# The projection slab of the decay rates two places earlier, its tables beside the last gate slabs, and the first convolution tap on ScalarE

## What is computed

```
hin  = x * (1 + scale) + shift                      # adaLN
proj = hin @ w_in                                   # 1024 -> 3072 (q,k,v) + 1024 (gate z) + 8 (b) + 8 (a)
qkv, hist = causal_dwconv(proj[:3072], conv_hist, conv_w)     # 4 taps per channel, over time
q, k, v = split(silu(qkv));  q, k = l2_normalize(q)/sqrt(128), l2_normalize(k)
beta = sigmoid(b);  g = -exp(a_log) * softplus(a + dt_bias)   # the rates, per token and head
G = cumsum(g) in each chunk                                   # decays: exp(G), exp(G_last - G), exp(G_i - G_j)
per chunk: solve (I + A) u = ..., with A from beta, k k^T and the decays; update the state S; o = ...
o = rms_norm(o) * silu(z);  out = o @ w_out
```

## Time and profile before

| | us |
|---|---|
| median of the runs | 3310.03 |
| the profiled execution's own time | 3313.34 |
| its span | 3311.8 |
| PE busy in it | 3096.9 (94%) |
| DVE busy | 1899.9 (57%) |
| ACT busy | 1074.6 (32%) |
| POOL busy | 925.7 (28%) |

### The profile page before, as it was taken

How to read it: one execution, slowest core, us unless ns; L and a number is a source line. 1 busy time by engine, 2 the same in 40 slices (tenths; PEclk the granted TensorE clock), 3 DMA queues, 4 the chain that set the end, 5 groups by cost and what they waited for, 6 DMA issues and landing times. The chain is left out here.

```text
span 3311.8 us, 51171 instructions
## 1 busy us (share of the span) xinstructions
PE 3096.9 (94%) x18908; PEld 2889.9 (87%) x18908; DVE 1899.9 (57%) x2897; ACT 1074.6 (32%) x2084; POOL 925.7 (28%) x648
## 2 busy tenths in 40 slices
PE   6999987999999999999998979989799999999995
PEld 2999985999988999999997867767789999999994
DVE  3899974777636545555547654434255555454555
ACT  1222223555426222222223634333144222222224
POOL 0322224566323322222222121010214222222222
PEclk8999997999999999999999989999899999999998
DMA  4444562221111111111110110000201111111111
GB/s 203 167 166 165 195 239 98 62 57 38 39 37 34 46 50 44 44 44 44 44 44 28 53 46 26 27 33 20 92 26 45 45 44 44 44 44 44 44 38 54
DMA packets 85016, 220.28 MB, mean 67 GB/s; under 512 B 9244, under 2 KB 40804, under 8 KB 83748
## 3 DMA queue, kind: packets, MB, share of 16 engines
q1 hardware_dynamic: 40692, 137.05, 12.3%
q10 hardware_dynamic: 44208, 81.66, 7.5%
HBM read 189.94 MB, written 28.75 MB: 66 GB/s over the span
## 5 line engine op out<-in xcount | busy, mean ns | idle before, releaser
L334 PE MATMUL PS<-HH,WH 128*128 128x354 f32 (+1 forms) x3336 | 1098.9, 329 | 78.7 <-issue 21.4
L338 PE MATMUL PS<-HH,WL 128*128 128x354 f32 (+1 forms) x3336 | 1091.1, 327 | 0.0
L337 PE MATMUL PS<-HL,WH 128*128 128x354 f32 (+1 forms) x3336 | 1090.4, 327 | 0.0
L330 POOL TENSOR_TENSOR WL<-RAW,WH 128x1024 fp32r<-128x1024 f32 x193 | 508.8, 2636 | 1054.5 <-ACT WH L325 1054.5
L334 PEld LDWEIGHTS PS<-HH,WH 128*128 128x128 f32 x3336 | 636.4, 191 | 94.4 <-issue 79.3
L337 PEld LDWEIGHTS PS<-HL,WH 128*128 128x128 f32 x3336 | 636.6, 191 | 1.8
L338 PEld LDWEIGHTS PS<-HH,WL 128*128 128x128 f32 x3336 | 635.0, 190 | 0.0
L1790 DVE SCALAR_TENSOR_TENSOR X<-PS,ADA,X 128x354 f32<-128x354 f32 (+1 forms) x704 | 329.8, 491 | 438.0 <-PE PS L338 437.5
L325 ACT ACTIVATE WH<-RAW 128x1024 fp32r<-128x1024 f32 x199 | 211.0, 1060 | 544.0 <-PE PS L334 543.7
L334 PE MATMUL PS<-FH,WH 128*128 128x354 f32 (+1 forms) x960 | 326.5, 340 | 9.9 <-DVE X L1790 9.8
L1765 DVE SCALAR_TENSOR_TENSOR CF<-UF,PSF,CF 128x1060 f32<-128x1060 f32 x176 | 331.6, 1939 | 0.0
(11 more groups left out here) (298 smaller groups left out, 4206.3 us busy)
## 6 DMA issues: line engine op xcount, KB each, us to landing
RAW<-ws SPq DMA_DIRECT2D x199, 512.0 KB, 3.6
ADR<-wada ACTq DMA_DIRECT2D x72, 512.0 KB, 4.9
scr<-V ACTq DMA_DIRECT2D x32, 530.0 KB, 3.6
AD<-wada SPq DMA_DIRECT2D x4, 2048.0 KB, 23.8
X<-xT SPq DMA_DIRECT2D x1, 4240.0 KB, 17.2
OUTT<-scr SPq DMA_DIRECT2D x1, 4240.0 KB, 14.6
scr<-OH ACTq DMA_DIRECT2D x8, 530.0 KB, 2.7
ADG<-wada SPq DMA_DIRECT2D x2, 2048.0 KB, 11.5
```

Of the source, the lines that this page charges most:

```text
L330: e.tensor_tensor(WL[u][:, :], RAW[:, u, :], WH[u][:, :].bitcast(fp32), ALU.subtract).then_inc(lo_done, 1)
L334: mm = e.matmul(out, WH[w][:, c:c + 128], mh, start=first, stop=False)
L337: e.matmul(out, WH[w][:, c:c + 128], ml, start=False, stop=False)
L338: return e.matmul(out, WL[w][:, c:c + 128], mh, start=False, stop=last)
```

## The change

Four things, all in the first 600 us.

1. **The first tap.** ACT computes CV = U·w0 (an activation Copy with the tap as scale) right after it has copied U and before it splits WH. DVE keeps the other three taps.
2. **The order of slabs.** The b and a slab is put at place 30; the last two gate slabs are 31 and 32. The tables are made under slabs 31 and 32: PE's transposes stand between the first and second chunk of slab 31, its sums between the same chunks of slab 32, the GCN transpose ahead of the last chunk of slab 32. The banks of the tables change (5, 6, 7 and 3). The order of ACT, DVE and POOL follows.
3. **Loads.** SP also issues KF and QE of chunk 2, ahead of gsc and ADG; ACT no longer does at chunk 0. The gsc store stands ahead of ADG. The load of S0 by ACT is put after the GAM activations of chunk 0, and both it and `vec_init(0)` wait for the stores of the last gate slabs.
4. **Places in SBUF**: AB over U, GTR a tile of its own.

```diff
+S_AB = QKVB + ZB - 2
...
             load_kq(sp, 1)
+            load_kq(sp, 2)
+            sp.wait_ge(gx, 9)
+            sp.dma_start(gsc, GTR[0:8 * (GT + 1), :]).then_inc(gt_st, 16)
             need(sp, up_done, 3 * (QKVB + ZB) + 3)
...
-                        if i + 2 <= LAST:
+                        if 1 <= i <= LAST - 2:
                             load_kq(a, i + 2)
...
+                    if not z:
+                        need(act, pst_rdy, n + 1)
+                        need(act, up_ev, 3 * n + 3)
+                        act.activation(CV[u][:, :], UB[u][:, GAP - (GC - 1):GAP - (GC - 1) + T], ACT.Copy, scale=PST[:, u, 0:1]).then_inc(tap_rdy, 1)
...
+            load_ada(act, S_AB, 0, True)
             for ch, (c0, cw) in enumerate(CHS):
-                need(act, up_done, 3 * n + ch + 1)
+                need(act, up_done, 3 * S_AB + ch + 1)
                 act.activation(AB[:, c0:c0 + cw], PS[:, ch, 0:cw], ACT.Copy).then_inc(up_ev, 1)
+                if ch == 0:
+                    load_ada(act, S_AB + 1, 1, True, 3)
+            split_hi(act, S_AB + 2, 0)
...
-                    v.tensor_scalar(CV[u][:, :], src(0), PST[:, u, 0:1], None, ALU.mult).then_inc(vec_ch, 1)
...
+            vec_ada_sums(v, S_AB, 0, S_AB // 2, True)
...
             v.tensor_tensor(GX[:, 1], GX[:, 1], GX[:, 3], ALU.subtract).then_inc(bg_rdy, 1)
+            vec_ada_sums(v, S_AB + 1, 1, S_AB // 2, True)
             need(v, gx, 4)
...
+            def to_tokens(ch):
+                if ch == 1:
+                    need(pe, up_ev, 3 * (S_AB + 1))
...
+                if ch == 2:
+                    need(pe, gx, 1)
+            dense(pe, S_AB + 1, 1, S_AB + 1, 1, to_tokens)
+
+            def decays(ch):
+                if ch == 1:
+                    need(pe, bg_rdy, 6)
...
+                if ch == 2:
+                    pe.wait_ge(bg_rdy, 9)
...
+                    pe_gt(pe)
+            dense(pe, S_AB + 2, 0, S_AB + 2, 0, decays)
```

More of the change, by code:

```diff
@@ L1199, in act_gdn @@
             act_gam(a, 0, 1)
+            for u in range(2):
+                need(a, v_st[u], 16 * (QKVB + ZB) // 2)
+            a.dma_start(SS0[:, :, :], s0).then_inc(s0_ld, 16)
             act_vb(a, 0)
@@ L1376, in vec_gdn @@
             vec_aq(v, 0)
+            for u in range(2):
+                need(v, v_st[u], 16 * (QKVB + ZB) // 2)
             vec_init(v, 0)
@@ L2565, in _, with gate @@
                 body(i, False)
-            with act.Fori(QKVB // 2, (QKVB + ZB) // 2 - 1) as i:
+            need(act, tail_rdy, QKVB)
+            act.dma_start(o_gcv, TAIL[:, :, :, :]).then_inc(out_done, 16)
+            with act.Fori(QKVB // 2, S_AB // 2) as i:
                 body(i, True)
-            body((QKVB + ZB) // 2 - 1, True, True)
-            n = QKVB + ZB
+            def gate(n, u, b):
+                need(act, v_st[u], 16 * (b // 2))
+                for ch, (c0, cw) in enumerate(CHS):
+                    need(act, up_done, 3 * n + ch + 1)
+                    act.activation(VV[u][:, c0:c0 + cw], PS[:, 3 * u + ch, 0:cw], ACT.Silu).then_inc(up_ev, 1)
+                need(act, up_ev, 3 * n + 3)
+                act.dma_start(scr[b, :, :], VV[u][:, :]).then_inc(v_st[u], 16)
@@ L2571, in _ @@
+            load_ada(act, S_AB, 0, True)
             for ch, (c0, cw) in enumerate(CHS):
-                need(act, up_done, 3 * n + ch + 1)
+                need(act, up_done, 3 * S_AB + ch + 1)
                 act.activation(AB[:, c0:c0 + cw], PS[:, ch, 0:cw], ACT.Copy).then_inc(up_ev, 1)
+                if ch == 0:
+                    load_ada(act, S_AB + 1, 1, True, 3)
+            split_hi(act, S_AB + 2, 0)
             need(act, ab_ps, 1)
-            act.activation(BETAG[:, :, 8:16], PS[:, 0, 0:(GT + 1) * 16].rearrange("p (t c) -> p t c", c=16)[:, :, 0:8], ACT.Sigmoid).then_inc(gx, 1)
+            need(act, bg_rdy, 1)
@@ L2577, in _ @@
+            act.activation(BETAG[:, :, 8:16], PS[:, B_AB, 0:(GT + 1) * 16].rearrange("p (t c) -> p t c", c=16)[:, :, 0:8], ACT.Sigmoid).then_inc(gx, 1)
+            act.activation(AL[:, :], PAR[:, P_ALOG:P_ALOG + 8], ACT.Exp).then_inc(gx, 1)
             need(act, bg_rdy, 4)
             act.activation(GX[:, 2], GX[:, 1], ACT.Exp).then_inc(gx, 1)
-            need(act, gx, 2)
+            need(act, gx, 3)
             act.activation(GX[:, 2], GX[:, 2], ACT.Ln, bias=1.0).then_inc(gx, 1)
-            act.activation(AL[:, :], PAR[:, P_ALOG:P_ALOG + 8], ACT.Exp).then_inc(gx, 1)
@@ L2582, in _ @@
[L2582 to L2585, removed]
+            gate(S_AB + 1, 1, S_AB)
             act.wait_ge(out_done, 16)
             act.wait_ge(bg_rdy, 9)
-            act.activation(EGN[:, :], PS[:, 1, 0:8 * (GT + 1)], ACT.Exp).then_inc(gx, 1)
-            act.activation(EGL[:, :], PS[:, 2, 0:8 * (GT + 1)], ACT.Exp).then_inc(gx, 1)
+            act.activation(EGN[:, :], PS[:, B_ADA, 0:8 * (GT + 1)], ACT.Exp).then_inc(gx, 1)
@@ L2590, in _ @@
+            act.activation(EGL[:, :], PS[:, B_ADA + 1, 0:8 * (GT + 1)], ACT.Exp).then_inc(gx, 1)
             act.activation(EKD[:, 8:], EKD[:, 8:], ACT.Exp).then_inc(gx, 1)
             act.activation(EKD[0:DEC, 0:8], EKD[0:DEC, 0:8], ACT.Exp).then_inc(gx, 1)
-            act.wait_ge(gx, 8)
+            act_gt(act)
+            gate(S_AB + 2, 0, S_AB + 1)
+            act.wait_ge(gx, 9)
             act_gdn(act)
@@ L2688, in _ @@
             v.wait_ge(g_ini, 1)
+            need(v, ada_sum, QKVB + ZB)
+            vec_ada_constants(v, 1, NSUB)
+            v.wait_ge(ada_done, ADA_LGB + 2)
             vec_gdn(v)
@@ L2749, in pack @@
     win[:, :A["gdn_w_in"].shape[2]] = A["gdn_w_in"][0]
-    put(S_A, cols(win))
+    win = cols(win)
+    put(S_A, np.concatenate([win[:S_AB], win[-1:], win[S_AB:-1]]))
     put(S_WO, cols(A["gdn_w_out"][0]))
```

71 lines of the change are left out of this document (29 added, 42 removed).

## The result

The changed kernel took 3277.99 us (median of 4 runs, 3276.32 to 3279.32), the kernel before 3309.74 beside it (4 runs, 3308.85 to 3312.19): a ratio of 0.9902, 95% interval 0.9887 to 0.9917. The profiled execution took 3277.79 with a span of 3276.0. The forecast was 3274, its range 3263 to 3288. The whole was right within 4 us, but each of its four terms was off by 1.4 to 3.5, one upwards and three downwards. That is what the experiments are about.

A forecast was written before the change was run, and what follows sets the result against it. PE, busy for 94% of the span, was taken as the bound, so only its idle stretches could give time back. Gains of 13.5 + 10.4 + 3 + 9.5 = 36.4 us led to 3274 us, range 3263 to 3288.

The forecast's parts named there:

- The first tap: Projection: moving the tap to ACT cuts PE's waits for WL; gain 13.5 us, or 16 if the ring is 11.7 or less.
- the ring: Per slab, V's silu, U's copies, ACT's tap, DVE's three taps: 12.05 us against PE's 11.72, with 5.7 us of slack left.
- PE begins to wait at slab 20: Projection: slack used up after 17 slabs; with the later slabs and some tenths at slab 26, 2.5 us still lost.
- The tables: End of projection: the 14.0 us stretch goes, less 2.6 of PE work and 1.0 of waits; gain 10.4, bounds 7.5 and 11.4.
- 1.0 for both waits: Slabs 31 and 32: PE's waits for ACT's sigmoid and for BETAG together cost 1.0 us, bounds 0 and 4.
- The start of chunk 0: From chunk 0's first transposes: PE stays at the higher clock; gain 3 us, bounds -1 and 4.6.
- that term of nothing: Start of chunk 0: ADG and GB of chunk 1, issued as late against it as before, cost nothing.
- The wait of 12.65 us: Chunk 2: QE's wait goes, ACT then waits 3 us for GB; gain 9.5 us, bounds 8 and 12.65.
- A ring of 12.4 to 12.6: Rival, projection: ring not shortened enough, conv gives 0 to 7 us; 3283 us in all, chance 0.16.
- PE alone bounds the projection: Rival, projection and chunk 2: PE sets the projection's pace and GB comes in time; 3266 us, chance 0.10.
- The late transfer that only changes its name: Rival, chunks 0 and 2: GB lands later or chunk 0 waits for ADG; last two terms 4 us, 3282, chance 0.08.
- Slower (WL blocks two taps): Rival, projection: WL blocks two of DVE's three taps by 2.0 us each, ring 14.1; 3321 us, chance 0.04.

The follow-up runs named there:

- longer ring: The changed kernel with a second ScalarE activation of the tap's size, into a scratch tile, ahead of the tap: 3302.21 us, ratio 0.9970.
- early load: The changed kernel with one more unused 8-column sigmoid on ScalarE ahead of its wait for VectorE's first rate op: 3275.25 us, ratio 0.9896.
- filled waits: The changed kernel with GB of chunk 2 loaded ahead of OUTT and 33 unread matmuls in PE's waits in chunk 0: 3266.86 us, ratio 0.9868.
- all four edits: The changed kernel with rates' transposes in bank 2, BETAG behind two sums, GB ahead of OUTT and the extra early sigmoid: 3264.60 us, ratio 0.9859.
- GB first: The changed kernel with SyncE's load of GB for chunk 2 ahead of that of OUTT: 3268.89 us, ratio 0.9874; run again, 3270.54 us.

## Why the prediction was right, and where it was not

**The first tap: 13.5 forecast, 17.0 measured, above the bound of 16.** The mechanism was right in each link. The first tap hid no second block (6.05 us for three taps), the ring is slower than PE, and its slack runs down. The size was off, in two numbers. The ring turns in 11.92 us, not 12.05; and PE's own slab is 11.67 (338.33 for slabs 2 to 30), not 11.72, which also makes the loss of before larger, 17 instead of 16. In the ring's sum the 0.15 for ACT's wait on its own copies, which no row had shown, was too much: the copies that began at 209.86 ended at 210.08 and the tap began at 210.11. At 11.92 the lag grows by 0.25 a slab. The slack was about the 5.7 that I had worked out: WL of slab 3 ended at 107.53, 6.1 before that slab (113.66); WL of slab 25 ended at 369.73, 0.6 before that slab (370.32). So it just lasted, and the step "PE begins to wait at slab 20" failed. The longer ring shows that this was a matter of tenths: 1.04 us a turn more cost 23.9 us in slabs 2 to 30.

**The tables: 10.4 forecast, 7.6 measured.** From the start of slab 31 (440.32, before 456.56) to the first transposes it was 29.9 us after 37.5. The failed term is "1.0 for both waits": the one ahead of slab 31 was 3.00, the one in slab 32 nothing. I had put the end of DVE's set 30 at 7 to 9 us behind slab 30; it came at 9.8, since WL of slab 32 fell on one of its sums. And I had counted all table loads as hidden. This one begins when the wait for DVE ends and is ahead of PE's last chunk with its 1.28 us; the early load takes it away there, but brings back 0.94 in slab 32, so it was one of two chains of nearly the same length. The clock is the other part: it fell in this gap (0.72 for 452.10 to 457.60), and with filled waits, where it didn't, the same stretch is 28.5 us, 1.4 less. That profile also gives the small matmuls and the restarts: 28.5 less two slabs and 3.0 of wait is 2.2, where I had 2.6, of which the 0.25 for a restart stood in no row. With all four edits slab 31 to chunk 0 is 4.4 us shorter, which is the whole of the wait and the clock together.

**The start of chunk 0: 3 forecast, 1.6 measured.** I had asked for the clock to stay up. It didn't: it was low again 5.5 us behind the first transposes (0.63 for 470 to 491). Of the 1.6 us, 1.5 came up to K of chunk 1 (16.8 us, from 470.19 to 486.97, after 18.3, from 494.07 to 512.34): the transposes of KF took 1.04 instead of 1.92, and those of QE 1.03, and began 4.3 us behind the first ones instead of 5.4. The mask ran at the low clock, behind a wait of 0.46 for the activation that follows the new table load (474.36). With PE's waits filled and the clock up all through, the stretch to K of chunk 1 was no shorter (17.2), and what the clock gave came behind it. From before to the filled waits the whole stretch loses 3.9 us, so the 4.6 could not be had by the clock even so. PE waited for neither ADG nor GB there, so that term of nothing was right.

**The wait of 12.65 us: 9.5 forecast, 7.7 measured, just under the bound of 8.** QE's wait and VF's long issue went, and GB's landing took their place, as forecast. The failed term is GB's landing: ACT waited 6.32 instead of 3. In the time of before (issue at 538.35, now at 512.89, so 25.46 added) GB was there at 555.2, not at "553", 16.8 us behind its issue; and ACT wanted it at 548.9, not at 549.5 to 550.8. The megabyte less in flight had not brought it forward: it took 1.1 us longer than the 15.7 of before. Both ends of "8 to 12.65" were off as well: 14.5 could be had, with GB first.

**The sum.** 17.0 + 7.6 + 1.6 + 7.7 = 33.9, against 36.4; the marks give 34.1, with 0.1 in slabs 0 and 1. The medians give 31.75 and the two profiled executions 35.5; the spread of the last 2480 us is wide enough for both. Errors of +3.5, -2.8, -1.4 and -1.8 partly cancelled, so the closeness of 3274 to 3278 is in part luck and says less for the working than it seems. Of the signs that I had named, the clock at chunk 0 failed after 5.5 us, the slabs of 12.0 us behind slab 20 never came, and the wait in slab 31 was at the 3 us that I had set as wrong.

**The rivals.** A ring of 12.4 to 12.6 was wrong by 0.5 us a turn. "PE alone bounds the projection" was right in that half, and wrong in the other (GB). The late transfer that only changes its name was true of nearly half of that stage, 6.7 of 14.5 us. Slower (WL blocks two taps) is excluded by the 6.05.

## What to carry to other kernels

Where engines pass a buffer round, price the ring and its slack, not the busy share: a ring 0.25 us slower than the bound cost nothing in 22 turns, and one 1.3 us slower cost 24 us, with the engine that was made slower busy for under half of the time. When a load is moved up, look for the next one that its consumer needs and for what stands ahead of that in its queue, since a reorder of two loads was worth nearly as much as the move itself. And compare versions a few microseconds apart between marks in the trace ahead of the parts that vary from run to run, but look at the granted clock between the marks first: here one kernel differed from itself by 1.6 us in one stretch.

## What the runs showed that I had not expected

- The table load stood behind the wait of its activation: it began when the wait ended (450.55) and held up that activation by 1.28 us; an activation of 8 columns ahead of the wait moved it to 442.24.
- With 33 matmuls whose output nobody reads, put into PE's waits, the granted clock was 1.00 all through and the stretch 1.5 to 3.1 us shorter (one profile, against two of the kernel without them).
- The same gap of 3.0 us ahead of slab 31 was followed by a fallen clock in some profiles and not in others: slab 31's last chunk to the decays took 9.3 us after the change and 10.6 with GB first, and 7.9 with GB first and filled waits, with the same instructions on PE up to there.
- A sum of DVE with WL beside it took 2.0 us longer, as a tap does (3.23 here, 1.23 at 205.33 above):

```profile
444.05 3.23 DVE L752 CUSTOM_DVE_ANT_0 PS<-ADR,CB 128x1024 f32<-128x1024 f32 x1
```

The Trainium skill, "SBUF — State Buffer", § Who interferes with whom, has a DVE instruction with two inputs in SBUF and a GpSimd one that reads SBUF exclude each other for a whole instruction. By that rule the price is what was left of WL when the sum was started, and the trace agrees: WL ran from 443.44 to 446.20, so 2.15 us were left at 444.05, and the sum took 2.0 longer.

All four edits together with the filled waits were not tried, so whether these gains add stays open. Why the clock stayed up behind the 3.0 us gap in one profile and fell in others stays open too, and so does the length of the low stretch in chunk 0.
